# FNet layer 0 of a diffusion backbone: tokens transformed first, and all sixteen modulations of the second shift and scale as TensorE matmuls

## Chip, cores and metric

One core of a Trainium2 chip. The number that counts is the device time of one execution in microseconds (us). The kernel is written directly against the engines: TensorE (PE), VectorE (DVE), ScalarE (ACT), GpSimd (POOL), and SyncE (SP), which issues the large transfers. Each engine runs its own list of instructions in order and waits on semaphores.

## The reference

One inference step of a four-layer backbone on 128 context tokens and 512 latent tokens, 1024 channels, float32. Every layer is a token mixer (layer 0: Fourier, 1: pooling, 2: latent attention, 3: Fourier) followed by a gated ConvFFN. Both halves of a layer are modulated:

```
for i in range(DEPTH):
    sh1, sc1, g1, sh2, sc2, g2 = split(silu(cond) @ w_ada[i] + b_ada[i], 6)   # for c_ctx and for c
    h = rms_norm(x) * (1 + sc1) + sh1
    x = x + g1 * mixer_i(h)          # mixer 0: real part of FFT over (tokens, 256 channels), then @ w_fnet
    h = rms_norm(x) * (1 + sc2) + sh2
    x = x + g2 * conv_ffn(h, w_ffn_in[i], w_ffn_conv[i], b_ffn_conv[i], w_ffn_out[i])
```

Each of the six vectors has 1024 values, eight pieces of 128. So a layer has 48 *modulation units*: one unit is 128 outputs of `silu(cond) @ w_ada`, for both conditionings, and needs 512 KB of `w_ada`.

## The kernel before

`x` lies in SBUF channels by tokens (`x[128, 8, 644]`). All weights come through one stream of 512 KB units into a ring of four slots `raw0..raw3` (SP, L423 and L428). Unit n+4 is loaded once unit n was given back (`unit_done`), in the order of the stream. The products are float32 made of three TensorE passes: each operand is split into a rounded part `_hi` (ACT) and the rest `_lo` (POOL for weights, `cut`, L441; DVE for the others), and `product` (L563) issues hi*hi, hi*lo and lo*hi.

A modulation unit is computed in one of two ways. On DVE, `modulate` (L1802) multiplies the unit with `cond` and sums, once for each conditioning. On PE, `modulation` (L784, and the same loop inline at L1039) does eight matmuls of two columns each against `cond_columns`. DVE's output is added in place, PE's is copied from PSUM (`copy_modulations`).

Layer 0 runs in these stages, each engine's list written out by hand:

1. Sixteen units for shift and scale 1 (ten on DVE, six on PE) while DVE and ACT sum the squares of `x`. Then the statistics, and the normalised, modulated tokens `h_hi`, `h_lo` (`norm_half`).
2. `fnet`: PE does twelve units at once, "pe" units of the stream, before its first product. Then the channel transform of ten pieces (`STAGE1_ORDER`, outputs `freq`), and the token transform of nine pieces (`FOLDED`, outputs `folded`), with four more "pe" units between them and eight "dve" units on DVE.
3. The *fold projection*: eight steps m. DVE adds and subtracts two halves of a weight unit (`fold_unit`, L1910 and L1911), ACT rounds it, DVE makes the rest (`fold_lo`), PE does 27 passes (nine tiles of three, 324 or 320 columns), DVE updates `x` (`update_folded`, L1760). After each step PE does one "last" modulation unit (the eight of SC2).
4. The ConvFFN: 22 pairs of tiles in three parts of 8, 8 and 6 pairs, each part followed by a projection. With each pair DVE computes two modulation units of the next layer, and four more in the projection of part 1 (`EXTRA_PART`, `project_with_units`). All 48 units of layer 1 are made this way.

```
def fnet_units(layer):
...
        units += pe[:12]
...
    for m in range(KC):
        units += [("fold", m)] + ([("pe", MODS - LAST_PE + m)] if late else [])
```

Layers 1 to 3 and the ends of the program are not touched but for names.

## Time and profile before

| | us |
|---|---|
| median of 3 runs (2883.63 to 2891.56) | 2885.51 |
| the profiled execution | 2884.26 |
| its span, first to last instruction | 2882.5 |
| PE busy | 2637.6 (92%) |
| DVE busy | 1609.0 (56%) |
| ACT busy | 917.0 (32%) |
| POOL busy | 846.6 (29%) |

The profiled execution spends 1.8 us outside its span. The page gives each engine's busy time and the chain of work that ended last: 63% of it is on PE. PE's granted clock has two levels, shown as 1.00 (2.4 GHz) and 0.50 (1.2 GHz). The layers after the first FFN of this program do not differ between the two kernels, so the reading below stays with the first 250 us.

### The profile page before, as it was taken

The page shows a single profiled execution, that of the slowest core. Times are in us where ns is not written, and L with a number is a line of the kernel's source. Part 1 is how long each engine was busy: PE and PEld are TensorE (multiplying, and loading weights), DVE is VectorE, ACT ScalarE, POOL GpSimd, SP SyncE. Part 2 cuts the span into 40 slices and gives each one's busy share as a digit, 9 for nine tenths or more (in the row PEclk, how much of TensorE's full clock was granted, in tenths as well). Part 3 has the DMA queues.
Part 4 walks back from the last instruction along what each step waited for, and adds up shares of the span by engine and source line. Part 5 has one row for each costly group of instructions (what it writes and reads, how often), then busy time and mean ns, then how long its engine had stood idle before and what let it go on. Part 6 is the DMA issues. An engine that isn't in the chain of part 4 may idle for free.

```text
span 2882.5 us, 45477 instructions
## 1 busy us (share of the span) xinstructions
PE 2637.6 (92%) x17182; PEld 2589.7 (90%) x17182; DVE 1609.0 (56%) x2705; ACT 917.0 (32%) x1368; POOL 846.6 (29%) x414
## 2 busy tenths in 40 slices
PE   6889999996399999998888999999999888999997
PEld 6879999996399999988887889999999887999997
DVE  7478546576875475763543344754757776323235
ACT  3133223133332231343322333332323434323232
POOL 0012333334423333422111012233333302333332
PEclk9989999998699999999988899999999999999999
DMA  7433334342033343422100012333434311222222
GB/s 261 144 135 124 131 102 148 123 149 91 29 130 126 115 148 119 151 90 78 44 30 30 30 44 74 111 135 104 146 122 141 97 66 59 73 78 75 73 73 74
DMA packets 83858, 293.44 MB, mean 102 GB/s; under 512 B 9952, under 2 KB 13472, under 8 KB 83360
## 3 DMA queue, kind: packets, MB, share of 16 engines
q1 hardware_dynamic: 77184, 281.05, 28.9%
q10 hardware_dynamic: 6560, 10.79, 1.1%
q8 instruction: 81, 1.33, 0.2%
q14 instruction: 33, 0.27, 0.0%
HBM read 288.88 MB, written 2.93 MB: 101 GB/s over the span
## 4 chain that ended last, share of the span: by engine, by line
PE 63%; issue 16%; DVE 9%; POOL 5%; ACT 3%; DMA 2%; ACTq 0%; POOLq 0%; SPq 0%; DVEq 0%
PE acc L563 58%; POOL w_lo L441 4%; PE sacc L563 3%; PE sacc L784 2%; DMA raw<-in_stream 2%; DVE x L1760 1%; DVE rows L1789 1%; DVE pt_lo L1677 1%; POOL res_ffn L441 1%; DVE rows L1635 1%; POOL w_next L441 1%; DVE rows L1628 1%; DVE rows L1709 1%; DVE x L1700 1%; PE acc L980 1%
## 5 line engine op out<-in xcount | busy, mean ns | idle before, releaser
L441 POOL TENSOR_TENSOR w_lo<-raw,w_hi 128x1024 fp32r<-128x1024 f32 (+3 forms) x317 | 710.1, 2246 | 1729.4 <-ACT w_hi L1070 1729.4
L563 PE MATMUL acc<-h_hi,w_hi 128*128 128x322 f32 x2880 | 907.8, 315 | 90.9 <-DVE x L1780 28.6
L563 PE MATMUL acc<-h_lo,w_hi 128*128 128x322 f32 x2880 | 902.7, 313 | 0.0
L563 PE MATMUL acc<-h_hi,w_lo 128*128 128x322 f32 x2880 | 901.8, 313 | 0.0
L563 PEld LDWEIGHTS acc<-h_hi,w_hi 128*128 128x128 f32 x2880 | 549.6, 191 | 101.2 <-issue 77.4
L563 PEld LDWEIGHTS acc<-h_lo,w_hi 128*128 128x128 f32 x2880 | 552.5, 192 | 0.2
L563 PEld LDWEIGHTS acc<-h_hi,w_lo 128*128 128x128 f32 x2880 | 549.1, 191 | 0.0
L1070 ACT ACTIVATE w_hi<-raw 128x1024 fp32r<-128x1024 f32 (+2 forms) x283 | 293.0, 1036 | 784.7 <-PE acc L563 744.5
L1802 DVE SCALAR_TENSOR_TENSOR products<-raw,cond 128x1024 f32<-128x1024 f32 x324 | 440.5, 1396 | 12.2 <-ACT cond L1557 8.2
L1854 DVE SCALAR_TENSOR_TENSOR conv<-acc,conv_w,conv 128x644 f32<-128x644 f32 x168 | 149.4, 889 | 371.6 <-ACT conv L1293 267.8
L563 PE MATMUL acc<-g_hi,w_hi 128*128 128x322 f32 x1120 | 350.3, 313 | 5.8 <-POOL w_lo L441 5.8
L563 PE MATMUL acc<-g_hi,w_lo 128*128 128x322 f32 x1120 | 346.8, 310 | 0.0
L563 PE MATMUL acc<-g_lo,w_hi 128*128 128x322 f32 x1120 | 346.5, 309 | 0.0
L1780 DVE SCALAR_TENSOR_TENSOR x<-acc,mod,x 128x128 f32 (+5 forms) x198 | 74.9, 433 | 299.5 <-PE acc L563 299.5
L563 PEld LDWEIGHTS acc<-g_hi,w_hi 128*128 128x128 f32 x1120 | 210.5, 188 | 7.1 <-POOL w_lo L441 6.8
L563 PEld LDWEIGHTS acc<-g_lo,w_hi 128*128 128x128 f32 x1120 | 212.6, 190 | 0.3
L563 PEld LDWEIGHTS acc<-g_hi,w_lo 128*128 128x128 f32 x1120 | 210.9, 188 | 0.0
L1858 DVE SCALAR_TENSOR_TENSOR conv<-acc,conv_w,conv 128x644 f32<-128x644 f32 x168 | 149.4, 889 | 24.6 <-DVE conv L1854 22.2
L1298 ACT ACTIVATE g_hi<-gated 128x644 f32 (+1 forms) x88 | 65.4, 743 | 279.3 <-DVE gated L1864 279.3
L563 PE MATMUL acc<-g_hi,res_ffn 128*128 128x322 f32 x576 | 131.2, 311 | 6.1 <-DVE x L1700 6.1
L1868 DVE TENSOR_TENSOR g_lo<-gated,g_hi 128x644 f32 (+1 forms) x88 | 75.6, 859 | 88.8 <-ACT g_hi L1298 88.8
L1289 ACT ACTIVATE gated<-conv 128x644 f32<-128x644 f32 x88 | 65.7, 747 | 181.1 <-DVE conv L1858 181.1
(210 smaller groups left out, 3709.1 us busy)
## 6 DMA issues: line engine op xcount, KB each, us to landing
raw<-in_stream SPq DMA_DIRECT2D x536, 512.0 KB, 3.3
x<-in_x ACTq DMA_DIRECT2D x8, 322.0 KB, 10.2
cond<-in_cond ACTq DMA_DIRECT2D x2, 1024.0 KB, 5.8
inv_count<-in_inv_count ACTq DMA_DIRECT2D x1, 1328.0 KB, 5.7
out_y<-y ACTq DMA_DIRECT2D x2, 644.0 KB, 4.2
out_y<-y ACTq DMA_DIRECT2D x8, 161.0 KB, 2.5
rows<-in_rope ACTq DMA_DIRECT2D x1, 644.0 KB, 3.9
conv_w<-in_conv_w ACTq DMA_DIRECT2D x4, 88.0 KB, 2.3
```

Source lines behind the costliest of these rows:

```text
L441: done = nc.gpsimd.tensor_tensor(lo[:, cols], raw[slot][:, cols], hi[:, cols].bitcast(f32), ALU.subtract)
L563: done = nc.tensor.matmul(o, lhs[lp], rhs[rp][half], start=first and z == 0, stop=last and z == 2)
L784: done = nc.tensor.matmul(sacc[1][:, 0, 2 * column:2 * column + 2], raw[u % SLOTS][:, k * P:(k + 1) * P], cond_columns[:, k, :], start=k = ...
L980: done = nc.tensor.transpose(acc[p][:, z // 4, (z % 4) * P:(z % 4 + 1) * P], probs[(5 * hh + t) % 2][:, z * P:(z + 1) * P], ident[:])
L1070: nc.scalar.activation(hi, raw[slot][:, 0:size], ACT.Copy).then_inc(weights_hi, 1)
L1289: nc.scalar.activation(gated[:], conv[0][:, 1:W + 1], ACT.Silu).then_inc(silu_done, 1)
L1298: nc.scalar.activation(g_hi[:, ds(gate, 1), :].rearrange("p o t -> p (o t)"), gated[:], ACT.Copy).then_inc(g_rounded, 1)
L1780: done = nc.vector.scalar_tensor_tensor(xs, acc[pair][:, bank, p0:p0 + x1 - x0], gate(cond_), xs, ALU.mult, ALU.add)
L1802: nc.vector.scalar_tensor_tensor(out[z][:], raw[slot][:], 1.0, cond[:, z, :], ALU.mult, ALU.mult, accum_out=mod[:, layer % 2, ds(index, 1) ...
L1854: nc.vector.scalar_tensor_tensor(to, halves(banks[half]), tap(0), to, ALU.mult, ALU.add).then_inc(left_done, 1)
L1858: nc.vector.scalar_tensor_tensor(to, halves(banks[half]), tap(2), to, ALU.mult, ALU.add).then_inc(result_taken, 1)
L1868: nc.vector.tensor_tensor(g_lo[:, gc, :].rearrange("p o t -> p (o t)"), gated[:], g_hi[:, gc, :].rearrange("p o t -> p (o t)").bitcast(f32 ...
```

## The change

Layer 0 gets its own stream (`FIRST_UNITS`) and its own function on each engine (`first_fnet`); `fnet` remains for layer 3.

- Tokens also arrive tokens by channels (five units "token"). ACT squares, sums and rounds them, DVE takes the reciprocal and the rest: `token_hi`, `token_lo`. The token transform is done first, on normalised tokens without modulation, in eight tiles c (24 passes of 258 or 256 columns and 6 of 66 or 64 each). Scale 1 is applied when the result is taken out of PSUM (`g_hi`, `g_lo`); shift 1 enters only the zero frequency (`zero_freq`).
- The channel transform comes second, in nine tiles (eight of 6 passes, one of 24).
- Units: PE does 30 as before, now SC1 (8), two of SH1, four of G1, and all sixteen of SC2 and SH2, two ahead of each fold step. DVE does ten ahead of the FFN (was eighteen). The eight of G2 move to DVE in the FFN of layer 0, and push eight of layer 1's into more places: four in the projection of part 0, eight in that of part 1.
- The transfers of `x` and of the small constants are issued by ACT after the first three token units, no longer first. The Nyquist weights come by a DMA of their own.

```
-    for m in range(KC):
-        units += [("fold", m)] + ([("pe", MODS - LAST_PE + m)] if late else [])
+def first_units():
+    units = [("token", 1), ("table", 0), ("table", 1), ("token", 2), ("token", 3), ("table", 2), ("token", 4),
+             ("token", 0)]
+    units += pe(*range(SC1, SC1 + 4))
+    for j in range(4):
+        units += pe(SC1 + 4 + j) + dve(SH1 + j)
+    units += dve(SH1 + 4, SH1 + 5) + pe(SH1 + 6, SH1 + 7)
+    for j in range(4):
+        units += dve(G1 + 4 + j) + pe(G1 + j)
+    units += [("fold", m) for m in range(3)]
+    for m in range(KC):
+        units += pe(SC2 + m, SH2 + m)
+        units += [("fold", m + 3)] if m + 3 < KC else []
...
+EXTRAS = {0: {0: 4, 1: 8}, 1: {1: 4}, 2: {1: 4}}
...
+            def first_fnet():
+                pe.wait_ge(cond_ready, 1)
+                wait_unit(first_place("table", 0))
+                wait_unit(first_place("table", 1))
+                for t in T_ORDER:
+                    ...
+                    wait_unit(first_place("token", t))
+                    for c in range(3):
+                        token_tile(c, t)
+                    if t == 3:
+                        modulation(SC1, 0, 0)
+                    if t == 4:
+                        modulation(SC1 + 1, 0, 1)
+                modulation(SC1 + 2, 1, 0)
+                modulation(SC1 + 3, 1, 1)
+                for c in range(3, KC):
+                    pe.wait_ge(result_taken, c - 2)
+                    for t in T_ORDER:
+                        token_tile(c, t)
+                    if c < KC - 1:
+                        if c % 2:
+                            pe.wait_ge(mods_taken, c // 2)
+                        modulation(SC1 + 1 + c, (c + 1) // 2 % 2, (c + 1) % 2)
+                pe.wait_ge(mods_taken, 3)
+                modulation(SH1 + 6, 0, 0)
+                modulation(SH1 + 7, 0, 1)
+                for i, j in enumerate(C_ORDER):
+                    ...
+                    if i < 4:
+                        if i == 0:
+                            pe.wait_ge(mods_taken, 4)
+                        modulation(G1 + i, 1, i)
+                def late(m):
+                    if m == 0:
+                        pe.wait_ge(mods_taken, 5)
+                    modulation(SC2 + m, 0, m)
+                    modulation(SH2 + m, 0, KC + m)
+                pe.wait_ge(nyquist_split, 1)
+                fold_project(0, 0, late)
...
+                for c in range(KC):
+                    if c % 2 == 0:
+                        take_modulations(SC1 + c, 2, c // 2 % 2, 0, True).then_inc(mods_taken, 1)
+                        dve.wait_ge(mods_taken, c // 2 + 1)
+                    take_tokens(c)
+                    if c >= 3:
+                        unit(SH1 + c - 3)
+                unit(SH1 + KC - 3)
...
+                squares(1)
+                first_table(0)
+                rounded(1)
+                first_table(1)
+                squares(2)
+                rounded(2)
+                squares(3)
+                rounded(3)
+                first_table(2)
+                for c in range(KC):
+                    act.dma_start(x[:, c, :], a["x"][c]).then_inc(loaded, 16)
...
+                squares(4)
+                rounded(4)
```

The diff shows, in this order, the stream, PE's `first_fnet`, and the cores of DVE's and of ACT's.

**The fold step on PE.** The end of one step and the start of the next; `acc<-folded,w` are the products, `sacc1<-cond_columns,raw` is a modulation unit. Before:

```order
L563 MATMUL acc1<-folded0_52,w_hi1_59 128x320
L563 MATMUL acc1<-folded1_53,w_hi1_59 128x320
L563 MATMUL acc1<-folded0_52,w_lo1_61 128x320
L784 MATMUL sacc1<-cond_columns_69,raw3_57 128x2 x8
L563 MATMUL acc0<-folded0_52,w_hi0_58 128x324
L563 MATMUL acc0<-folded1_53,w_hi0_58 128x324
```

Changed:

```order
L635 MATMUL acc0<-folded0_52,w_hi0_60 128x320
L635 MATMUL acc0<-folded1_53,w_hi0_60 128x320
L635 MATMUL acc0<-folded0_52,w_lo0_62 128x320
L857 MATMUL sacc1<-cond_columns_74,raw2_58 128x2 x8
L857 MATMUL sacc1<-cond_columns_74,raw3_59 128x2 x8
L635 MATMUL acc1<-folded0_52,w_hi1_61 128x324
L635 MATMUL acc1<-folded1_53,w_hi1_61 128x324
```

Two units stand between two steps where one stood.

**The channel transform on PE**, changed kernel, from the end of its second tile (`acc0`) to the start of its third (`acc1`):

```order
L635 MATMUL acc0<-g_hi_86,tables0_101 128x320
L635 MATMUL acc0<-g_lo_87,tables0_101 128x320
L635 MATMUL acc0<-g_hi_86,tables1_102 128x320
L857 MATMUL sacc1<-cond_columns_74,raw3_59 128x2 x8
L635 MATMUL acc1<-g_hi_86,tables0_101 128x320
L635 MATMUL acc1<-g_lo_87,tables0_101 128x320
```

Each of the first four tiles has six such passes, and a unit follows it. Before, a piece of this transform had twelve passes of 256 columns, and a unit came after every fourth piece.

**ACT's first instructions**, before:

```order
L1567 DMA cond<-in_cond 128x2048
L1568 DMA cond_columns<-in_cond_columns 128x16
L1569 DMA b_ada<-in_b_ada 128x96
L1571 DMA x<-in_x 128x644 x8
L1573 DMA ident<-in_ident 128x128
L1573 DMA ones<-in_ones 128x128
L1573 DMA perm<-in_perm 128x128
L1573 DMA gains<-in_gains 128x26
```

Changed, from the rounding of the third token unit on (`token_lo,token_sum<-raw` is the squaring, `token_hi<-raw` the rounding):

```order
L1470 ACTIVATE token_hi<-raw_56,token_rstd 128x1024
L1194 ACTIVATE tables_101<-raw_57 128x650
L1490 DMA x<-in_x 128x644 x8
L1492 DMA ident<-in_ident 128x128
L1492 DMA ones<-in_ones 128x128
L1492 DMA perm<-in_perm 128x128
L1492 DMA gains<-in_gains 128x26
L1462 ACTIVATE token_lo,token_sum<-raw_58 128x1024
L1465 ACTIVATE token_rstd<-token_sum,eps 128x1
L1470 ACTIVATE token_hi<-raw_58,token_rstd 128x1024
```

The twelve issues of `x` and the constants stood in the first rows; they now stand ahead of the fourth token unit.

## Rows read from the trace of the kernel before

**Rows 1.** Busy time by stage: us, busy us and instructions of each engine, granted clock, DMA share, GB/s

```profile
91.40:136.40 45.00, 42.71 (x320) 42.25 (x320) 27.65 (x57) 10.14 (x28) 0.00 (x0) 0.92 0.38 130
...
145.30:193.10 47.80, 46.83 (x328) 46.68 (x329) 37.02 (x81) 12.49 (x14) 2.83 (x4) 0.95 0.46 161
193.10:209.20 16.10, 4.48 (x23) 3.08 (x22) 10.04 (x26) 6.60 (x12) 8.34 (x12) 0.64 0.29 98
...
507.00:563.00 56.00, 56.00 (x379) 56.00 (x379) 30.42 (x46) 9.23 (x9) 21.09 (x8) 1.00 0.35 114
```

**Rows 2.** Modulation units on PE: cold ones grouped (ns min/median/max), two warm ones

```profile
L784 PE MATMUL sacc<-cond_columns,raw x192: 345/352/373, 49.4 to 91.2; 128*128 128x2 f32 x192
...
151.46 1.84 PE L784 MATMUL sacc<-cond_columns,raw 128*128 128x2 f32 x16
...
157.24 1.84 PE L784 MATMUL sacc<-cond_columns,raw 128*128 128x2 f32 x16
```

**Rows 3.** Granted clock in four short stretches, same columns as rows 1

```profile
105.50:109.00 3.50, 2.85 (x25) 2.64 (x24) 3.50 (x9) 0.98 (x4) 0.00 (x0) 0.99 0.73 272
109.00:112.40 3.40, 3.40 (x18) 3.40 (x18) 2.09 (x4) 0.41 (x1) 0.00 (x0) 0.51 0.42 146
...
145.30:149.90 4.60, 4.58 (x17) 4.60 (x18) 2.43 (x3) 0.00 (x0) 0.00 (x0) 0.50 0.19 73
...
156.70:160.10 3.40, 3.40 (x29) 3.40 (x28) 1.73 (x3) 0.40 (x1) 0.00 (x0) 1.00 0.25 101
```

**Rows 4.** Timeline of PE: start, us, line, tiles, [idle before]

```profile
107.19 2.00 PE L784 MATMUL sacc<-cond_columns,raw 128*128 128x2 f32 x16 [0.66 <-DMA raw<-in_stream]
...
145.32 0.88 PE L563 MATMUL acc<-folded,w_hi 128*128 128x324 f32 x2 [8.89 <-issue]
```

**Rows 5.** Timeline of PE: passes of 256 columns, cold and warm

```profile
91.98 0.41 PE L563 MATMUL acc<-tables,h_lo 128*128 128x256 f32 x1
...
92.62 0.41 PE L563 MATMUL acc<-tables,h_lo 128*128 128x256 f32 x1
...
98.08 0.28 PE L563 MATMUL acc<-tables,h_lo 128*128 128x256 f32 x1
...
98.43 0.28 PE L563 MATMUL acc<-tables,h_lo 128*128 128x256 f32 x1
```

**Rows 6.** Timeline of ACT: two pieces of the token transform taken

```profile
118.97 0.44 ACT L1079 ACTIVATE folded<-acc 128x324 fp32r<-128x324 f32 x1 [1.32 <-PE acc L563]
...
120.74 0.44 ACT L1079 ACTIVATE folded<-acc 128x324 fp32r<-128x324 f32 x1 [1.32 <-PE acc L563]
```

**Rows 7.** Timeline of ACT (ACTq: its issues): the start, and the tables

```profile
2.17 4.34 ACTq L1571 DMA_DIRECT2D x<-in_x  x8
...
10.27 1.28 ACT L1556 ACT_TABLE_LOAD   x1 [10.27 <-issue]
...
45.60 2.64 ACT L1070 ACTIVATE tables<-raw 128x1024 fp32r<-128x1024 f32 x3 [4.23 <-DVE mod L1819]
```

**Rows 8.** Timeline of POOL: the rests of the three tables

```profile
46.73 6.18 POOL L441 TENSOR_TENSOR tables<-raw,tables 128x1024 fp32r<-128x1024 f32 x3 [46.28 <-ACT tables L1070]
```

**Rows 9.** DMA issues: KB each, median us from issue to landing

```profile
raw<-in_stream SPq DMA_DIRECT2D x536, 512.0 KB, 3.3
...
b_ada<-in_b_ada ACTq DMA_DIRECT2D x4, 48.0 KB, 3.6
...
cond_columns<-in_cond_columns ACTq DMA_DIRECT2D x1, 8.0 KB, 7.0
```

**Rows 10.** Chain that ended last, in order of time: one wait in the fold projection

```profile
177.77 5.63 DMA raw<-in_stream
```

**Rows 11.** Timeline of DVE: from the update of one fold step to the next fold unit

```profile
172.94 1.57 DVE L1760 SCALAR_TENSOR_TENSOR x<-acc,mod,x 128x65 f32<-128x65 f32 x5
...
177.13 0.68 DVE L1911 TENSOR_TENSOR sums<-raw 128x512 f32<-128x512 f32 x1
```

**Rows 12.** Timeline of ACT between the fold projection and the FFN

```profile
200.40 1.06 ACT L1070 ACTIVATE w_next<-raw 128x1024 fp32r<-128x1024 f32 x1 [3.21 <-DMA raw<-in_stream]
```

More of the change, by code:

```diff
@@ L146, in extra, with first_place, fnet_units, fnet_place @@
+FIRST_DVE = [u for kind, u in FIRST_UNITS if kind == "dve"]
+FIRST_MODS = G2
+assert N_FIRST % SLOTS == 0 and len(FIRST_PE) + len(FIRST_DVE) == FIRST_MODS
+def first_place(kind, i):
+    return FIRST_UNITS.index((kind, i))
+def fnet_units():
+    return [("table", j) for j in range(TABLE_UNITS)] + [("nyquist", 0)] + [("fold", m) for m in range(KC)]
+def fnet_place(kind):
+    return [u for u, (k, i) in enumerate(fnet_units()) if k == kind]
 def extra(layer, part):
-    return ADA_EXTRA if ada_in_ffn(layer) and part == EXTRA_PART else 0
+    return EXTRAS.get(layer, {}).get(part, 0)
@@ L472, in project @@
             def project(size, more):
-                places = [*WEIGHT_PLACES, 12, 13] if more else list(range(10))
+                places = WEIGHT_PLACES[more] if more else list(range(10))
                 for j in range(2, 10):
@@ L1873, in ffn @@
                     if part == 0:
[L1874 to L1876 removed]
+                        pair(0, 0, acc, layer == 0)
+                        pair(1 // turn, 1 % turn, sacc[::-1], layer == 0)
+                    start = 2 // turn if part == 0 else 0
+                    if part == 0 and layer == 0:
+                        for i in range(2, (MODS - FIRST_MODS) // 2):
+                            pair(i, 0, acc, True)
+                        start = (MODS - FIRST_MODS) // 2
+                    with dve.Fori(start, count // turn) as i:
                         for z in range(turn):
```

741 lines of the change are left out of this document (441 added, 300 removed).

## The prediction, made before the changed kernel ran

> **What bounds the kernel now.** I read the stages first, since only layer 0 changes. The FNet mixer takes 209 us before the FFN's first product. In the busy times by stage [rows 1] PE is full or nearly so in both transforms (42.71 of 45.0 us) and in the fold projection (46.83 of 47.8). The reader should see that PE is the engine to count, although a large part of its time in layer 0 is modulation units, eight matmuls of two columns each. The grouped row of L784 [rows 2] shows their price: the twelve units from 49.4 to 91.2 last 42 us, 3.5 us each, with no DMA or DVE in the way. In the fold projection the same unit lasts 1.84 us in the record and moves the list by 1.7 (a step is 157.24 - 151.46 = 5.78 us, 4.08 of products and 1.7 of a unit).
>
> The two prices are PE's two clocks. The granted clock [rows 3] is 0.5 from 109.0 to 112.4 and from 145.3 to 149.9. The passes of 256 columns show it directly: three take 92.62 - 91.98 = 0.64 us before 95 us and 98.43 - 98.08 = 0.35 later [rows 5]. (The clock column reads 1.00 before 95 us as well; the durations there are those of 1.2 GHz, so I go by the durations.) The clock rose after 3.9 us of products, not during 42 us of busy two-column matmuls. So a unit does not keep PE's clock up. One unit between long runs of products does no harm: at 156.7 to 160.1 the clock stays 1.00 [rows 3]. One unit and a gap of 0.66 us, at 107.19 [rows 4], cost it: it fell at 109.0 for 3.4 us. That is the fact on which this prediction turns.
>
> After the fold projection, 16.1 us pass to the FFN [rows 1], set by the transfer, on which ACT waits 3.21 us [rows 12]; nothing in this piece changes. From there on PE is full.
>
> **The sum.** It goes from the start to the last fold product (193.1 us now).
>
> *Start.* ACT issues three small transfers (2.1), loads a table (1.28, [rows 7]) and waits for `b_ada`: issued at 1.7 and 3.6 on the way [rows 9], so 5.3; with the 7.0 of `cond_columns` it would be 8. Then two issues, a second table load and the issue of `cond` bring it to 8. Squaring and root 1.4 (estimate: 2.64 us for 2698 columns of tables [rows 7] is 1.0 per 1024, and a little for the sum), a table 1.0: 10.4. POOL makes the rests of two tables at 2.3 each (6.18 for 2698 columns, [rows 8]). **First product at 16**, against 91.4. This is the gain: twelve cold units and the statistics no longer stand ahead.
>
> *Three token tiles, first part.* 54 passes, 18 cold at 0.213 and 36 at 0.118: 8.1 us, then a unit; 28. The fourth token unit is late. ACT reaches it at about 20 and then issues twelve transfers; at the start these took it from 2.17 to 10.27 [rows 7], 8.1 us. So 28; squaring 1.4, rounding 1.0 and DVE's rest 1.2 give **32**. PE waits 4 us for it and is cold again.
>
> *Rest of three tiles.* 18 wide passes cold 3.9, 18 narrow ones cold at 0.2, three units between 1.7 and 3.5, I take 8 for them: **47.5**. (Narrow, warm: a piece of the token transform is 12 wide and 3 narrow passes in 120.74 - 118.97 = 1.77 us [rows 6], less 12 x 0.118, leaves 0.11 each.)
>
> *Five tiles.* 24 x 0.118 + 6 x 0.11 = 3.5 each, and four units at 1.7: 24.3. A unit follows six narrow passes, so this is lighter than the fold step; I take three falls of the clock at 3.4 us and half speed, 1.7 each: **77**. Two more units, the second behind DVE's units in the ring: 8, **85**.
>
> *Channel transform.* Six passes of 320 columns are 0.9 us warm. Between single units there is too little, so cold: 6 x 0.27 + 3.5 = 5.1, four times, 20.4; four tiles without a unit, 5; the Nyquist tile, 24 passes, 4.5; small waits. **117**. The two transforms with their units thus end 19 us earlier than the 136.4 of now, and the folding of weights, 8.9 us of idle PE [rows 4], is done beside them: 28 us gained.
>
> *Fold projection.* Each step has 4.08 of products and now two units, 3.4: 7.5 us, 60 for eight, against 47.8. With 3.4 us of units in one piece I expect the clock to fall once a step. Price: the first step now, cold to 149.9, runs from 145.32 to 151.46, 6.14 instead of 4.08 [rows 2, 4]: 2.1 a step, 17. With 1 to 2 us of waits for the ring: **79**, so the last product at **196**, 3 us later than now.
>
> The bounds of this term: no fall gives 60; all units cold and each step's products as slow as the first's, 6.1 + 7.0 = 13.1, gives 105. I take one fall a step, since a single unit of 1.7 with a short gap already did it [rows 3, 4].
>
> The Trainium skill (TensorE: Matmul & The Clock Gate, "Why this matters for your kernels") asks, against drops of throughput, only that no long idle gaps stand between bursts of matmuls. PE is not idle here, and by that rule the clock would hold. The trace disagrees at 109.0. The rule's case is the first rival.
>
> *In the FFN.* DVE gets eight more units in layer 0, four in the projection of part 0 and four more in that of part 1. In part 1 DVE is busy 30.42 of 56 us with four units [rows 1]; four more at 2.4 make 40. PE covers it: nothing. Without that cover it would be at most 12 x 2.4 = 29 us. Copies and biases of the modulations, below 1 us each beside PE: nothing. SP's list has four units more before the FFN's end, in places where the ring waits anyway.
>
> Sum: +3 us on the profiled execution's 2884.26: **2887 us**. That execution lies 1.2 us under the median of the three runs.
>
> **Rivals.**
>
> *The clock holds (faster).* For it: it holds in the fold projection now, and the units still are matmuls. Against: rows 3 at 109.0. Then the channel transform is 4 x (0.9 + 1.7) instead of 20.4, minus 10; the falls of the five tiles, 5, are not paid, nor the 17 of the fold steps: 32 us less, 2855. If it holds in half the fold steps and the five tiles, minus 13: 2874.
>
> *The ring becomes the bound in the fold projection (slower).* Three units a step now pass through four slots, two before. The two units of step m+2 are loaded only when DVE gave back fold unit m+3, which is behind the update of x: 177.8 - 172.94 = 4.9 us after the products of step m [rows 11]. They land 3.3 us later if alone [rows 9], 5.6 as in the chain's wait at 177.77 [rows 10]. Two steps then take 4.9 + L + 7.5 us, a step 7.9 with L = 3.3 and 9.0 with 5.6. It decides from L = 2.6 on, when the clock is up; with a fall each step, 9.6, only when L exceeds 6.8 or the fall lies outside the wait. In the bad case both add: 9.0 + 2.1 = 11.1, 89 us, 10 more than my sum, and a second fall in the early tiles 2: 2899.
>
> *DVE's new units hold PE up in the FFN.* Up to 29 us, 2916. Against it the 16 us free in part 1. Small.
>
> *It does not start early.* If `b_ada` lands late and every token unit with it, the start moves by 3 to 5 us, but PE waits for the fourth token anyway. 2890, within the first case.
>
> **How the numbers follow.** About 0.3%, 8.7 us, is what a measurement of this kernel can tell from no change. The forecast, gain at the start given back by the fold projection, has 0.58: 2877 to 2894. The clock holding in whole or in half has 0.21, the ring 0.17, the FFN 0.04. Faster is 0.21, the same 0.58, slower 0.21. The range, 2868 to 2899, takes in the forecast, the half case and the usual price of the ring; the full case of the first rival and the far end of the others are left out.
>
> **What would show it.** Right: the first product near 16 us; a wait of PE of some 4 us before the fourth token; the transforms done near 117; granted clock 0.5 in one or more short stretches in each fold step, and a mean step of 9 to 10 us; the last fold product at 190 to 200; FFN unchanged. Wrong: a clock of 1.00 through the fold projection with steps of 7.5 to 8 us (first rival); idle PE ahead of the units with the ring named as releaser, longer than 1 us in each step (second); PE gaps at the projections of parts 0 and 1 (third).

## The result, and the profile after

| | changed | before |
|---|---|---|
| median of 20 runs | 2876.24 us (2868.0 to 2890.24) | 2886.8 us (2873.74 to 2892.93) |
| ratio, with 95% interval | 0.9975 [0.9963, 0.9987] | |
| profiled execution, span | 2875.66, 2873.9 us | 2884.26, 2882.5 us |

The changed kernel is 0.25% faster, by some 7 us going by the ratio. The forecast was 2887, no change. The time lies in the range, but on the side to which I gave 0.21.

The forecast was made of stages of layer 0, so these are read first. Busy time by stage of the changed kernel, with the columns of [rows 1]: three token tiles, five token tiles, channel transform, fold projection, the piece up to the FFN, and part 1 of the FFN.

```profile
15.80:49.60 33.80, 29.27 (x172) 28.79 (x173) 9.89 (x32) 16.09 (x28) 3.95 (x2) 0.75 0.77 265
49.60:84.00 34.40, 32.59 (x223) 32.51 (x222) 18.80 (x48) 7.54 (x21) 0.00 (x0) 0.75 0.37 123
84.00:118.30 34.30, 31.91 (x145) 31.54 (x145) 18.29 (x39) 5.63 (x11) 0.00 (x0) 0.56 0.61 214
118.30:198.50 80.20, 77.21 (x474) 76.24 (x472) 41.18 (x90) 13.03 (x15) 2.79 (x4) 0.79 0.44 148
198.50:212.10 13.60, 2.52 (x5) 1.24 (x5) 8.52 (x23) 6.52 (x12) 7.70 (x12) 0.67 0.15 56
510.10:566.30 56.20, 56.20 (x379) 56.20 (x378) 45.93 (x61) 9.24 (x9) 25.63 (x8) 1.00 0.44 151
```

The fold projection took 80.2 us where I had summed 79. PE's clock, 0.95 there before [rows 1], is 0.79. A mean of 0.79 between 1.00 and 0.50 is 42% of the 80.2 us at half speed, 34 us, and these cost half their length: 17 us, the term that I had put down for it. It came about in another way than I had it: the clock fell in five of the eight steps and not in all, and stayed low for 6.8 us each time. One such stretch, and one of the steps at full clock:

```profile
121.10:127.90 6.80, 6.80 (x28) 6.80 (x29) 2.99 (x4) 0.00 (x0) 0.00 (x0) 0.50 0.53 177
138.20:147.30 9.10, 9.10 (x71) 9.00 (x69) 5.59 (x12) 1.80 (x2) 0.00 (x0) 1.00 0.33 115
```

Lines of the timeline of PE in the changed kernel: the first product, the first unit, the first product of the fourth token, then in the fold projection two pairs of units (x32) and a single one (x16), and the first product of the FFN.

```profile
15.82 0.77 PE L635 MATMUL acc<-tables,token_hi 128*128 128x258 f32 x2 [15.82 <-POOL tables L501]
27.68 2.48 PE L857 MATMUL sacc<-cond_columns,raw 128*128 128x2 f32 x16 [2.68 <-DMA raw<-in_stream]
31.02 0.80 PE L635 MATMUL acc<-tables,token_hi 128*128 128x258 f32 x2 [0.86 <-DVE token_lo L2161]
...
118.34 4.33 PE L857 MATMUL sacc<-cond_columns,raw 128*128 128x2 f32 x32
129.02 4.74 PE L857 MATMUL sacc<-cond_columns,raw 128*128 128x2 f32 x32
...
148.18 1.95 PE L857 MATMUL sacc<-cond_columns,raw 128*128 128x2 f32 x16 [0.71 <-DMA raw<-in_stream]
...
212.06 0.61 PE L635 MATMUL acc<-h_hi,w_hi 128*128 128x322 f32 x1 [6.29 <-issue]
```

The FFN starts at 212.06, 2.87 us later than before, where 3 was forecast. So in this profile layer 0 did what I said, and the program still ended 8.6 us earlier. The gain lies far behind layer 0, in code that the change leaves as it was: at the statistics of layer 2's q (1366.05 us before, 1368.12 now) the changed kernel is still 2.1 us behind.

**Where it comes from.** The costliest groups of POOL, each form of instruction by itself (busy us, mean ns). First a second profile of the kernel before, then one of the changed kernel:

```profile
L441 POOL TENSOR_TENSOR w_lo<-raw,w_hi 128x1024 fp32r<-128x1024 f32 x249 | 640.3, 2572 | 1274.8 <-ACT w_hi L1070 1274.8
L441 POOL TENSOR_TENSOR res_ffn<-raw,res_ffn 128x768 fp32r<-128x768 f32 x24 | 47.6, 2013 | 4.2 <-ACT res_ffn L1070 4.2
L441 POOL TENSOR_TENSOR w_next<-raw,w_next 128x256 fp32r<-128x256 f32 x32 | 23.2, 759 | 13.7 <-ACT w_next L1070 13.7
L441 POOL TENSOR_TENSOR res_mla<-raw,res_mla 128x1024 fp32r<-128x1024 f32 x5 | 11.9, 2403 | 30.2 <-ACT res_mla L1070 30.2
```

```profile
L501 POOL TENSOR_TENSOR w_lo<-raw,w_hi 128x1024 fp32r<-128x1024 f32 x249 | 650.5, 2613 | 1265.9 <-ACT w_hi L1194 1265.9
L501 POOL TENSOR_TENSOR res_ffn<-raw,res_ffn 128x768 fp32r<-128x768 f32 x24 | 39.7, 1679 | 5.5 <-ACT res_ffn L1194 5.5
L501 POOL TENSOR_TENSOR w_next<-raw,w_next 128x256 fp32r<-128x256 f32 x32 | 20.3, 670 | 11.1 <-ACT w_next L1194 11.1
L501 POOL TENSOR_TENSOR res_mla<-raw,res_mla 128x1024 fp32r<-128x1024 f32 x5 | 9.9, 2015 | 38.6 <-ACT res_mla L1194 38.6
```

The same instructions on the same shapes: 2013 ns and 1679, 759 and 670, 2403 and 2015. Of these only `w_lo` did not become quicker. What differs is where the tiles lie. The change places three small tiles that I had read over, ahead of all tiles but `x`, `h`, `raw`, the four weight tiles and the small constants:

```
+        token_sum, token_rstd = place("token_sum", [P, 5]), place("token_rstd", [P, 5])
+        zero_freq = place("zero_freq", [P, 2, KC])
         g_at = at[0]
```

That is 26 words, 104 bytes. The sizes add up to a start of `g_hi`, and with it of `tables`, `res_mla`, `w_next` and four of the six `res_ffn`, at 60 modulo 64 bytes before and at 36 now. The other two `res_ffn` and `w_nyq` start at 28 before and at 4 now. `raw`, `w_hi` and `w_lo` start at 0 in both.

### The profile page after: what moved, and what is told of

It reads as the page before. It is cut to its first block, busy times and chain, and to the rows that moved or that the text cites. A ratio compares the mean times of both kernels' runs of the same rounds, so it can differ in the third digit from the quotient of the medians.

```text
span 2873.9 us, 45480 instructions
## 1 busy us (share of the span) xinstructions
PE 2643.5 (92%) x17235; PEld 2597.9 (90%) x17235; DVE 1593.3 (55%) x2692; ACT 918.8 (32%) x1369; POOL 840.7 (29%) x414
## 4 chain that ended last, share of the span: by engine, by line
PE 69%; issue 13%; DVE 9%; POOL 4%; ACT 3%; DMA 1%; ACTq 0%; POOLq 0%; DVEq 0%; SPq 0%
PE acc L635 63%; POOL w_lo L501 3%; PE sacc L635 3%; PE sacc L857 2%; DMA raw<-in_stream 1%; DVE x L1935 1%; DVE pt_lo L1853 1%; DVE rows L1804 1%; DVE rows L1811 1%; DVE rows L1964 1%; POOL w_next L501 0%; ACT w_hi L1194 0%; DVE scratch L2308 0%; DVE h_lo L1827 0%; POOL res_ffn L501 0%
## 5 line engine op out<-in xcount | busy, mean ns | idle before, releaser
L501 POOL TENSOR_TENSOR w_lo<-raw,w_hi 128x1024 fp32r<-128x1024 f32 (+3 forms) x317 | 719.4, 2274 | 1826.0 <-ACT w_hi L1194 1826.0
L1977 DVE SCALAR_TENSOR_TENSOR products<-raw,cond 128x1024 f32<-128x1024 f32 x304 | 428.4, 1446 | 2.6 <-issue 2.5
L1955 DVE SCALAR_TENSOR_TENSOR x<-acc,mod,x 128x128 f32<-128x128 f32 (+5 forms) x198 | 75.0, 434 | 269.0 <-PE acc L635 269.0
```

Of the source, the lines that this page charges most:

```text
L501: done = nc.gpsimd.tensor_tensor(lo[:, cols], raw[slot][:, cols], hi[:, cols].bitcast(f32), ALU.subtract)
L1955: done = nc.vector.scalar_tensor_tensor(xs, acc[pair][:, bank, p0:p0 + x1 - x0], gate(cond_), xs, ALU.mult, ALU.add)
L1977: nc.vector.scalar_tensor_tensor(out[z][:], raw[slot][:], 1.0, cond[:, z, :], ALU.mult, ALU.mult, accum_out=mod[:, layer % 2, ds(index, 1) ...
```

## The experiments

Sixteen more runs were made, three of them of the two kernels as they are. "Rest" is the time from the first FFN product to the end of the profiled execution's span. The expectations count to PE's last product instead, some 10 us less.

| kernel | median, us | ratio to before [95%] | FFN starts | rest |
|---|---|---|---|---|
| before, as above | 2886.8 | 1 | 209.2 | 2673.3 |
| changed, as above | 2876.24 | 0.9975 [0.9963, 0.9987] | 212.1 | 2661.8 |
| before_again | 2884.03 | 0.9992 [0.9981, 1.0003] | 211.5 | 2676.5 |
| before_pad4 | 2882.83 | 0.9992 [0.9982, 1.0002] | 209.3 | 2672.9 |
| before_pad128 | 2888.26 | 1.0004 [0.9993, 1.0015] | 214.4 | 2678.3 |
| after_old_places | 2885.16 | 0.9990 [0.9975, 1.0004] | 214.1 | 2682.2 |
| before_late | 2891.94 | 1.0015 [0.9998, 1.0032] | 213.8 | 2669.8 |
| before_pad (104 bytes) | 2879.54 | 0.9968 [0.9953, 0.9983] | 209.9 | 2673.9 |
| after_again | 2879.7 | 0.9973 [0.9959, 0.9987] | 212.1 | 2667.4 |
| after_third | 2875.44 | 0.9969 [0.9953, 0.9986] | 208.5 | 2663.4 |
| after_w32 | 2880.2 | 0.9981 [0.9965, 0.9998] | 209.5 | 2666.6 |
| after_late | 2883.01 | 0.9982 [0.9965, 0.9998] | 214.3 | 2677.3 |
| split_fold | 2888.21 | 1.0004 [0.9985, 1.0023] | 215.0 | 2668.0 |
| no_sh2 | 2871.71 | 0.9949 [0.9934, 0.9964] | 199.8 | 2661.6 |
| after_w36 | 2874.56 | 0.9966 [0.9952, 0.9980] | 210.1 | 2659.8 |
| before_w36 | 2873.32 | 0.9958 [0.9943, 0.9973] | 212.7 | 2659.0 |

The ratios are to the kernel before on the same chip, whose medians were 2885.4 to 2889.2. scan1 and scan2 were executed once each, for their profiles. A profile is one execution and its time lies where it may in the spread of 15 to 20 us: for the whole time the medians and ratios count.

### Is it scatter?

**before_again** and **after_again**: both kernels unchanged.

> The kernel before, unchanged, for the scatter of its parts. In the first pair of profiles layer 0 of the changed kernel ended 2.9 us later (first FFN product 212.06 against 209.19), and code that the change doesn't touch was 11 us shorter after it, 6 of them in layer 2's attention (1422 to 1556 against 1422 to 1561). Theory A (scatter): the granted clock falls in other places in each execution, so a second profile of the same kernel differs from the first by 3 us or more in attention and by 5 or more in all that follows 695 us. Theory B (real): two profiles of this kernel agree within 1.5 us in each of these, and the changed kernel is shorter there each time. Time ratio to before: 1.000 within 0.002.

> The changed kernel, unchanged, a second profile. Ratio to before 0.9975 again, within 0.0015. Theory A: its attention and layer 3 are not 6 and 5 us shorter than in the profiles of before, but anywhere between those of the two kernels. Theory B: 7 to 11 us shorter than before from 695 us on, again. Theory C (layer 0 quicker in most executions than in the one profiled): the first FFN product at 200 to 208 this time instead of 212.

The ratio came again, 0.9973, and before against itself gave 0.9992. The rest was 2676.5 and 2667.4. Theory C is out: the FFN started at 212.1 once more. Attention (1422 to 1561 us in the first profile) is the clearest piece. Between the same two products, in the first and the second profile of before, then of the changed kernel (columns of [rows 1]):

```profile
1422.10:1561.40 139.30, 121.78 (x737) 113.04 (x737) 50.66 (x127) 40.35 (x100) 15.56 (x8) 0.85 0.10 31
```

```profile
1424.70:1564.50 139.80, 122.25 (x736) 113.70 (x736) 50.71 (x127) 40.44 (x100) 15.55 (x8) 0.84 0.10 31
```

```profile
1424.00:1556.60 132.60, 114.92 (x737) 106.67 (x736) 50.49 (x127) 39.93 (x99) 15.56 (x8) 0.89 0.10 33
```

```profile
1424.30:1557.30 133.00, 115.00 (x737) 106.73 (x737) 50.55 (x127) 40.01 (x100) 15.57 (x8) 0.89 0.10 33
```

The work of DVE, ACT and POOL is the same; PE's busy time and clock differ. Theory A asked for 3 us between two profiles of one kernel here; it was 0.5 and 0.4. That looked like theory B. But a third profile of the changed kernel (after_third, below) took 136.4 us in this stretch, 3.8 more than the first.

### The place of the tiles

**before_pad**, no instruction differs from before:

```
+        place("pad", [P, 26])
         g_at = at[0]
```

> The kernel before with 104 unused bytes (26 words) placed in SBUF ahead of g_hi, so that all that lies behind (g, tables, res_ffn, w_next, the attention's tiles) moves to where the changed kernel has it; no instruction differs. In two profiles of each kernel POOL's rest of 768 columns of res_ffn took 2.01 us before and 1.68 after, that of 256 columns of w_next 0.76 and 0.67, of 1024 columns of res_mla 2.40 and 2.01, while w_lo took 2.57 and 2.61. The changed kernel adds three small tiles of 104 bytes at that place. Theory E (placement): POOL's times become the changed kernel's (1.68, 0.67, 2.01), the code from the first FFN product on takes 2651 to 2658 us instead of 2662 to 2666, attention (1422 to 1561) 133 instead of 139, and the median falls by 6 to 10 us, to 2875 to 2881. Rival (the tiles' places do nothing on the path; the gain comes with the new order of layer 0 and its units): POOL may be quicker, the median stays within 3 us of before.

**after_old_places**, the changed kernel with its three tiles behind all others:

```
-        token_sum, token_rstd = place("token_sum", [P, 5]), place("token_rstd", [P, 5])
-        zero_freq = place("zero_freq", [P, 2, KC])
...
+        end_at = at[0]
+        token_sum, token_rstd = (place(f"token_{n}", [P, 5], f32, end_at + 20 * j) for j, n in enumerate(("sum", "rstd")))
+        zero_freq = place("zero_freq", [P, 2, KC], f32, end_at + 40)
```

> The changed kernel with its three small tiles (token_sum, token_rstd, zero_freq, 104 bytes) placed at the end of the allocation, so that all other tiles lie where they lay before. Theory E: POOL's times become those of before (2.01, 0.76, 2.40), the time from the first FFN product on is 2662 to 2666 us, and the median rises to 2885 to 2892, by what my forecast for layer 0 says above before. Rival: the median stays at 2876 to 2881.

The groups of POOL in before_pad:

```profile
L442 POOL TENSOR_TENSOR res_ffn<-raw,res_ffn 128x768 fp32r<-128x768 f32 x24 | 39.6, 1678 | 5.8 <-ACT res_ffn L1071 5.8
L442 POOL TENSOR_TENSOR w_next<-raw,w_next 128x256 fp32r<-128x256 f32 x32 | 20.2, 669 | 13.8 <-ACT w_next L1071 13.8
```

104 unused bytes give the kernel before the changed kernel's POOL and 0.9968, all of the change's gain. The changed kernel with the old places has POOL's old times (2017 ns for `res_ffn`) and 0.9990: its interval holds 1. It also reaches into that of the changed kernel, up to 0.9987, so the ratio of this run alone decides nothing; the times set right for the clock, below, do. One part of the expectation failed: before_pad's attention took 136.1 us and not 133, and its rest was 2673.9, no shorter than the 2673.3 of before; the profiled execution, at 2885.63 us, lay 6 us above the median of its runs. The gain of before_pad is seen in the median of its twelve runs, not in its profile.

**before_pad4** and **before_pad128**: the same line with `[P, 1]` and `[P, 32]`.

> The kernel before with 4 unused bytes ahead of g_hi instead of 104. What lies behind starts at 60 modulo 64 bytes in the kernel before, at 36 in the changed kernel, and here at 0, as raw, w_hi and w_lo do. POOL's rest takes 2.57 us for 1024 columns of w_lo (0 against 0), 2.40 for res_mla (60 against raw's 0) and 2.01 with 36. Theory G (the place of POOL's operands relative to each other, modulo 64, sets its speed, worst where they are equal): res_mla takes 2.5 to 2.6 us here, res_ffn 2.05 to 2.2, w_next 0.76 to 0.79, and the median is that of before or up to 3 us above. Rival (a tile that starts off a 64-byte line is what costs): both become quicker than with 36, below 2.0 and 1.67, and the median falls by more than the 9.7 us of the 104 bytes.

> The kernel before with 128 unused bytes at the same place: everything behind moves, but keeps its 60 modulo 64. Theory G: POOL's times stay at those of before (2.40 for res_mla, 2.01 for res_ffn, 0.76 for w_next) and the median within 2 us of before. Rival (any move of these tiles by some hundred bytes does it, or the gain of before_pad is scatter): times or median as in before_pad, 2.01 / 1.68 / 0.67 or 6 to 10 us less.

Neither changed POOL's times (`res_ffn` 2024 ns in the first, `res_mla` 2405) nor the ratio, 0.9992 and 1.0004. So 104 bytes matter for what they do to the remainder, not for moving the tiles, and with these two runs the place of the tiles is shown as the cause of the gain. That POOL's speed carries it is likely, not shown by itself: DVE's busy time also fell in before_pad, to 1601.1 us from 1608.0 to 1609.6 in the five profiles of the kernel before with POOL's old times. But 0 was no worse than 60, and the distance as I had it in theory G is not all.

**after_w32**: 8 unused words ahead of `w_hi` and 8 ahead of `g_hi`.

> The changed kernel with 32 unused bytes ahead of w_hi, and 32 more ahead of g_hi: raw starts at 0 modulo 64, w_hi and w_lo at 32, the rest at 36 as in the changed kernel. Theory G: the rest of 1024 columns of w_lo takes 2.0 to 2.1 us instead of 2.61, all 249 of them 510 to 530 us instead of 651. PE's waits that end with w_lo, 27 us in the changed kernel's profile, shrink by a fifth to a third: 5 to 9 us less, 2867 to 2874 us, the fastest so far. Rival: w_lo stays at 2.5 to 2.6 (then the place of the output, or something else, decides), and the median within 2 us of the changed kernel.

**after_third**, run beside it: the changed kernel unchanged.

> The changed kernel once more, as the measure for after_w32 on the same chip. Ratio to before 0.9965 to 0.9985; from the first FFN product on 2651 to 2658 us in the profile, first product at 205 to 214.

`w_lo` stayed at 2606 ns, so 32 modulo 64 is not a quick place, and theory G fell. The median did not fall: 2880.2 beside 2875.44 for after_third, with intervals that overlap. after_third did what I expected: 2653.4 us from the first FFN product to PE's last one.

**scan1** and **scan2** put single tiles at many places within one program:

```
-        res_ffn = [[place(f"res_ffn{i}{p}", [P, 6 * P], f32r, res_at[i] + 24 * P * p) for p in range(2)] for i in range(3)]
+        res_ffn = [[place(f"res_ffn{i}{p}", [P, 6 * P], f32r, res_at[i] + 24 * P * p + ((0, 4), (28, 64), (64, 92))[i][p]) for p in range(2)] for i in range(3)]
...
+        mla_shift = (0, 4, 12, 28, 44)
-        res_mla = [[place(f"res_mla{i}{p}", [P, UNIT], f32r, e_at + 4 * UNIT * (2 * i + p)) for p in range(2)]
+        res_mla = [[place(f"res_mla{i}{p}", [P, UNIT], f32r, e_at + 4 * UNIT * (2 * i + p) + mla_shift[i]) for p in range(2)]
```

In scan2 the shifts of `res_ffn` are ((0, 28), (28, 32), (36, 64)) and `mla_shift` is (32, 36, 48, 52, 60).

> The changed kernel with single tiles shifted. Start modulo 64 bytes, rounded part and rest alike: the five res_mla at 36, 40, 48, 0 and 16. Of res_ffn, rounded part / rest: tile 0 at 36 / 40, tile 1 at 0 / 36, tile 2 at 36 / 0; tiles 3 to 5 as before. raw is at 0 throughout. Theory G (distance to raw): a time that grows smoothly towards 0 and 60, so 36 and 40 quick (2.0), 48 and 16 between, 0 slow (2.4). Theory H (only starts at 4 modulo 32, or modulo 16, are quick): 36 at 2.0, all others 2.4. For res_ffn: if the rounded part's place decides (it is read), tiles 0 and 2 stay quick (1.55 undisturbed) and 1 is slow (1.84); if the rest's (it is written), tile 1 is quick and the others slow; if both must be alike, all three are slow.

> As scan1 with other offsets: res_mla at 4, 8, 20, 24 and 32; res_ffn tile 0 at 36 / 0, tile 1 at 0 / 4, tile 2 at 8 / 36. Theory H: 4 and (if it is modulo 16) 20 quick at 2.0 us, the others 2.4. Theory G: 20, 24 and 32 quick, 4 and 8 slow.

Timeline of POOL in scan1. Five `res_mla`, start modulo 64 bytes 36, 40, 48, 0, 16:

```profile
1751.38 2.01 POOL L502 TENSOR_TENSOR res_mla<-raw,res_mla 128x1024 fp32r<-128x1024 f32 x1 [31.12 <-ACT res_mla L1195]
1753.35 2.00 POOL L502 TENSOR_TENSOR res_mla<-raw,res_mla 128x1024 fp32r<-128x1024 f32 x1
1755.31 2.39 POOL L502 TENSOR_TENSOR res_mla<-raw,res_mla 128x1024 fp32r<-128x1024 f32 x1
1757.66 2.39 POOL L502 TENSOR_TENSOR res_mla<-raw,res_mla 128x1024 fp32r<-128x1024 f32 x1
1761.45 2.40 POOL L502 TENSOR_TENSOR res_mla<-raw,res_mla 128x1024 fp32r<-128x1024 f32 x1 [1.39 <-ACT res_mla L1195]
```

And in scan2, at 4 and 8, at 20 and 24 (two in a line, 2.00 us each), and at 32:

```profile
1743.83 3.95 POOL L502 TENSOR_TENSOR res_mla<-raw,res_mla 128x1024 fp32r<-128x1024 f32 x2 [35.48 <-ACT res_mla L1195]
...
1747.74 3.95 POOL L502 TENSOR_TENSOR res_mla<-raw,res_mla 128x1024 fp32r<-128x1024 f32 x2
...
1754.88 2.40 POOL L502 TENSOR_TENSOR res_mla<-raw,res_mla 128x1024 fp32r<-128x1024 f32 x1 [3.19 <-ACT res_mla L1195]
```

Quick are 36, 40, 4, 8, 20, 24; slow are 48, 0, 16, 32, and 60 from the kernel before. Modulo 16 that is 4 and 8 quick, 0 and 12 slow. Theory H had the period but not the 8. The split tiles, scan1, tile 1 (rounded part at 0, rest at 36) and tile 2 (rounded part at 36, rest at 0) of `res_ffn`:

```profile
1228.58 2.44 POOL L502 TENSOR_TENSOR res_ffn<-raw,res_ffn 128x768 fp32r<-128x768 f32 x1
...
1233.11 1.54 POOL L502 TENSOR_TENSOR res_ffn<-raw,res_ffn 128x768 fp32r<-128x768 f32 x1 [2.10 <-ACT res_ffn L1195]
```

Tile 1 took 2.14 us in the changed kernel, tile 2 1.55. So the tile that is read decides, and where the result goes does not. scan2 agrees: rounded part at 0 slow (2.43), at 8 or 36 quick (1.54), wherever the rest was.

The Trainium skill (SBUF — State Buffer, Specifications (TRN2)) gives SBUF lines of 16 bytes and says that each crossing to a new line is paid for. The period of 16 found here agrees with such lines. Why 4 and 8 past the other input are quick and 12 is not, neither the page nor a run here tells.

**after_w36** and **before_w36**: 9 unused words ahead of `w_hi` and 7 (33 in before) ahead of `g_hi`.

> The changed kernel with w_hi and w_lo at 36 modulo 64 (36 unused bytes ahead of them, 28 ahead of g_hi, so that the rest keeps its 36). If the place of the tile alone decides, w_lo's rest of 1024 columns takes 2.0 us undisturbed instead of 2.40 (mean 2.2 instead of 2.61), the 256 columns 0.64 instead of 0.73, and PE's waits that end with w_lo (27 us) shrink by a fifth: 2869 to 2874 us. Rival: w_lo stays at 2.4 and the median at 2875 to 2880; or it becomes quicker and the median does not move, since the falls of the clock take it back.

> The kernel before with w_hi, w_lo and all behind them at 36 modulo 64. If the place decides and nothing else: quick rests throughout as in after_w36, and a median 5 us below that of the 104 bytes alone: 2870 to 2876. Rival: w_lo unchanged, 2877 to 2881.

```profile
L503 POOL TENSOR_TENSOR w_lo<-raw,w_hi 128x1024 fp32r<-128x1024 f32 x249 | 548.6, 2203 | 1364.6 <-ACT w_hi L1196 1364.4
L503 POOL TENSOR_TENSOR w_nyq<-raw,w_nyq 128x1024 fp32r<-128x1024 f32 x1 | 2.0, 2003 | 16.8 <-ACT w_nyq L1196 16.8
L580 POOL TENSOR_TENSOR w_nyq<-nyquist_raw,w_nyq 128x1024 fp32r<-128x1024 f32 x1 | 2.5, 2526 | 10.0 <-ACT w_nyq L1500 10.0
```

POOL works 102 us less on `w_lo`. The last two lines show that the distance of the two inputs counts and not the place of one: `w_nyq` starts at 4 modulo 64 in both. `raw` starts at 0, a distance of 4 modulo 16, and takes 2003 ns. `nyquist_raw` lies behind the new pad and starts at 36, a distance of 0 modulo 16, and takes 2526. In the changed kernel, where `nyquist_raw` starts at 0, the same instruction took 2147.

The time followed little. before_w36 has 2873.32 us, ratio 0.9958, and after_w36 2874.56, 0.9966; the changed kernel, run beside after_w32, had 2875.44, 0.9969. The intervals overlap, so no order among these three is shown. Both medians lie below every median with the old places, and before_w36 does it without the change to layer 0.

### How a quicker POOL reaches PE

Some of it is direct. Ahead of layer 3: DVE, POOL and PE in the second profile of before, then POOL and PE in before_pad:

```profile
2288.89 2.81 DVE L1651 SCALAR_TENSOR_TENSOR h_lo<-rows,mod,h_hi 128x128 fp32r<-128x128 f32 x2
```

```profile
2288.95 4.95 POOL L441 TENSOR_TENSOR tables<-raw,tables 128x1024 fp32r<-128x1024 f32 x2 [27.57 <-ACT tables L1070]
```

```profile
2295.41 0.56 PE L563 MATMUL acc<-tables,h_hi 128*128 128x256 f32 x2 [4.33 <-issue]
```

```profile
2286.20 4.18 POOL L442 TENSOR_TENSOR tables<-raw,tables 128x1024 fp32r<-128x1024 f32 x2 [29.13 <-ACT tables L1071]
```

```profile
2291.88 0.61 PE L564 MATMUL acc<-tables,h_hi 128*128 128x256 f32 x2 [3.65 <-issue]
```

A pair of DVE's instructions that takes 0.67 us elsewhere takes 2.81 while POOL makes the tables' rests, and with POOL's 4.18 instead of 4.95 PE waits 0.68 us less. The Trainium skill (SBUF — State Buffer, Who interferes with whom) says that a VectorE instruction with two inputs in SBUF and a GpSimd one that reads SBUF keep each other waiting. The trace agrees.

Some goes by the clock. Behind POOL's rests of `w_next` PE waited 2.20 us at 1804.63 in before and 1.80 at 1809.17 in before_pad. Right behind that wait the clock fell in the one and held in the other. First before, then before_pad, the columns of [rows 1]:

```profile
1805.50:1808.70 3.20, 3.20 (x14) 3.20 (x14) 3.17 (x3) 0.53 (x1) 1.21 (x2) 0.50 0.00 0
```

```profile
1810.10:1813.30 3.20, 3.20 (x24) 3.20 (x23) 3.00 (x3) 0.51 (x1) 0.88 (x2) 1.00 0.00 0
```

PE did 14 matmuls in one and 24 in the other. The two executions differ in more than this wait, but the other profiles say the same. In all six with the old places (before, before_again, before_pad4, before_pad128, before_late, after_old_places) PE waited 2.18 to 2.21 us here and the clock fell right behind it. In the twelve others it waited 1.75 to 1.80, and the clock fell in one only, scan1. The fall lasts 3.4 us, so it costs at most 1.7.

*How much is clock.* The record has the mean granted clock of every execution. An estimate from it: time x (1 - clock) is what the low clock can have cost at most, and time x clock is the rest, which no fall of the clock can explain. In means, against the kernel before in the same session, with 95% intervals:

| | time, us | clock's part | the rest of it |
|---|---|---|---|
| before_pad | -10.1 | -5.8 ± 4.2 | -4.3 ± 1.6 |
| before_pad4 | -2.4 | -3.6 ± 2.2 | +1.2 ± 1.5 |
| before_pad128 | +2.8 | +1.9 ± 3.3 | +0.9 ± 1.5 |
| before_w36 | -12.1 | -5.0 ± 4.2 | -7.1 ± 1.4 |
| after_again | -6.9 | +35.9 ± 3.3 | -42.8 ± 1.2 |
| after_third | -8.2 | +33.8 ± 4.7 | -42.0 ± 1.2 |
| after_old_places | -2.8 | +36.2 ± 4.8 | -38.9 ± 1.6 |
| after_w36 | -9.9 | +36.3 ± 4.5 | -46.2 ± 1.6 |

The changed kernel has more low clock in layer 0, and the column shows the kernel before at 1.00 during its twelve cold units, so the rows of the changed kernel are read against each other only. In both kernels the new places take 3 to 4 us off the part without the clock, and `w_lo` at 36 takes off some 3 to 4 more. These differences are clear of the scatter. What the clock adds to it is 6 us in before_pad, with a wide interval, and is not seen in the changed kernel.

**before_late** and **after_late** test how far shifts alone move the clock's falls; before the statistics of q, 8 and 2 times

```
+                    nc.tensor.matmul(sacc[0][:, 0, 0:2], ones[:], sum_q[:, 0:2], start=True, stop=True)
```

> The kernel before with eight matmuls of two columns more (2 to 3.4 us) ahead of the statistics of q in layer 2 (near 1369 us), so that attention starts so much later. Theory F (where PE's clock falls depends on small shifts of the program): in both profiles of before the clock falls at 1423 and 1447 and in none of the four of the changed kernel, though the code is the same. With the shift these falls go or move: attention, 139 us from 1422 to 1561, becomes 132 to 136, and the added 2 to 3.4 us cost nothing in sum or bring a gain. Rival: attention stays at 139 within 1 us, and the whole time rises by the added 2 to 3.4 us.

> The changed kernel with two matmuls of two columns more (0.4 to 0.9 us) at the same place. Theory F: the program stood just on the good side of a fall, and so small a shift brings the falls at 1423 and 1447 back: attention 137 to 140 us instead of 132.5, the median up by 4 to 7 us. Rival: up by 0.4 to 0.9 us, attention as in the changed kernel.

Attention in before_late and in after_late:

```profile
1429.90:1562.90 133.00, 115.12 (x736) 106.70 (x735) 50.52 (x127) 40.02 (x99) 15.56 (x8) 0.89 0.10 33
```

```profile
1430.80:1571.40 140.60, 123.47 (x735) 114.83 (x735) 50.60 (x127) 40.26 (x99) 15.59 (x8) 0.83 0.09 31
```

The stretch took 140.6 us with two matmuls more, after 133 in the changed kernel, and 133.0 with eight more, after 139.5 in the kernel before. That looks like theory F, but it does not show it. Both executions came to the added matmuls some 6 us later than the first profile of their kernel: at 1372.03 against 1366.05, and at 1373.97 against 1368.12, where the additions themselves moved the list by 1.95 and 0.87 us. What else differed before them may have moved the falls. What is shown is that unchanged code takes 132.6 to 140.6 us here, by where the clock falls, so this stretch alone could not have told placement from luck. Nor does it stand for the whole: after_third, with nothing added, took 136.4 us in it, and before_w36, the fastest by its rest, 139.1. The medians moved little: after_late, 0.9982 against 0.9969 to 0.9975, is 2 to 4 us slower than the changed kernel where I expected 4 to 7, within what the intervals allow. before_late is 2.7 us above its before, which is the rival's 2 to 3.4, and no gain. An edit made to hit a good moment in one profile did not carry over to all executions.

### The units in layer 0

**split_fold**, the unit of SH2 within the step:

```
                         for z, j in enumerate(tiles):
+                            if layer == 0 and (part, z) == (0, 4):
+                                modulation(SH2 + m, 0, KC + m)
...
                     modulation(SC2 + m, 0, m)
-                    modulation(SH2 + m, 0, KC + m)
```

> Changed kernel, but in each fold step the unit of SH2 stands after the fourth of the nine tiles of products and only that of SC2 between two steps. My reading (PE's clock falls once a step because 3.6 us of units stand in one piece): pieces of 1.8 us between 2 us of products keep 1.00, a step is 4.1 + 3.6 = 7.7, or up to 8.8 where the ring binds, against 10.0; layer 0 ends 10 to 18 us earlier, the time falls by 10 to 18 us against the changed kernel (2858 to 2866). Rival (the clock falls with every unit, however short the piece, or the ring binds at once): a step stays at 9.5 to 10.5, the time within 4 us.

Two stretches of its fold projection:

```profile
122.00:158.40 36.40, 36.40 (x156) 36.40 (x154) 11.89 (x27) 4.24 (x5) 0.00 (x0) 0.50 0.36 130
```

```profile
182.00:197.00 15.00, 15.00 (x119) 15.00 (x118) 8.89 (x22) 3.48 (x4) 2.02 (x3) 1.00 0.56 182
```

And units of its timeline in each:

```profile
121.87 3.41 PE L857 MATMUL sacc<-cond_columns,raw 128*128 128x2 f32 x16
...
135.95 3.41 PE L857 MATMUL sacc<-cond_columns,raw 128*128 128x2 f32 x16
...
186.03 1.84 PE L857 MATMUL sacc<-cond_columns,raw 128*128 128x2 f32 x16
...
193.59 1.84 PE L857 MATMUL sacc<-cond_columns,raw 128*128 128x2 f32 x16
```

Neither theory held throughout. With the clock up, the same unit of two neighbouring steps stands at 186.03 and 193.59, a step of 7.56 us, as in my reading. With the clock down, 121.87 to 135.95, a step is 14.08. The clock fell in the first step, at 120.8, stayed low for 37.5 us and rose at 158.3 amid the same pattern; it fell once more at 168.6, behind a single unit before which PE had waited 0.46 us for the ring, for 10.2 us. What made it rise at 158.3 no run shows. The FFN started at 215.0, and the median, 2888.21, is 8 to 10 us above the changed kernel's by the ratios. In these two profiles, one of each, the pairs of the changed kernel lost the clock more often, five times, but for 6.8 us each; the single units lost it twice, and for longer: mean clock 0.79 against 0.71 over the projection. So the unbroken products of a step were worth more than short pieces of units.

**no_sh2**:

```
-                for k in range(KC):
+                for k in range(KC - 1 if SH2 <= unit < SH2 + KC else 0, KC):
```

> Changed kernel, but each unit of SH2 is one matmul instead of eight: seven eighths of these outputs' sums are left out (of the matmuls, k = 0 to 6). Prices the second unit of a fold step. My reading: without it the clock holds, a step is 4.1 + 1.8 + 0.2 = 6.1 us and the ring binds at some 7 to 8: layer 0 ends 16 to 28 us earlier. Rival (no fall of the clock is tied to the pair): a step loses only the unit's 1.8 or less, 14 us. In both the whole time should fall by what layer 0 loses; if it falls by less, the layers behind it give it back.

The FFN started at 199.8, 12.3 us earlier, less than I expected and near the rival's 14. Two pairs of its timeline:

```profile
137.00 3.72 PE L857 MATMUL sacc<-cond_columns,raw 128*128 128x2 f32 x18 [2.58 <-DMA raw<-in_stream]
...
154.84 4.00 PE L857 MATMUL sacc<-cond_columns,raw 128*128 128x2 f32 x18 [2.43 <-DMA raw<-in_stream]
```

With the second unit's work gone the ring is the bound. Behind each of these two gaps the pair ran at the low clock: 3.72 and 4.00 us, where it takes 2.06 at full clock. By the ratios the whole kernel became 6 to 8 us faster than the changed one (0.9949, from six runs, against 0.9969 to 0.9975) for the 12.3.

## Why the prediction was right and wrong

*Right, in the profile it was made for.* First product 16, measured 15.82. The fourth token at 32, measured 31.02; PE waited there 3.5 us in two pieces, 2.68 for a late unit and 0.86, for the 4 that I gave it. Five tiles to 77, measured 78.4 (the unit behind them starts there). Transforms done at 117, measured 118.3. Fold projection 79, measured 80.2, with the clock at 0.79. FFN at 212, measured 212.06. In part 1 DVE is busy 45.93 us, where I estimated 40, and PE is full, so the four more units there cost nothing.

*Right sums of wrong terms.* Part of this agreement is luck. The five tiles began early, at 45.9 and not 47.5, and took 32.5 us and not 29.4: the clock was low in five stretches and not three. In the fold projection I had eight falls at 2.1 us each, 17 in all; there were five of 6.8 us at half speed, at 3.4 each, 17 in all. The sign "granted clock 0.5 in one or more short stretches in each fold step" was therefore not seen: three steps held 1.00.

*The rivals.* The first, that the clock holds, came true in three steps of eight and gained nothing, since each fall lasted longer. The ring (second rival) cost PE four waits of 0.65 to 0.84 us, 2.9 in all, where my sum has 1 to 2; it became the bound only in no_sh2. The third, DVE in the FFN, cost nothing: from the first FFN product to the start of the next layer's statistics (694.25 before, 695.25 now) the changed kernel needs 483.2 us, before 485.1.

*Wrong.* The step that failed is "Sum: +3 us on the profiled execution's 2884.26": it takes all that lies behind layer 0 as unchanged. What stands ahead of the prediction says that the layers after the first FFN do not differ. Their instructions and the order of these are indeed the same; the tiles they work on had moved by 104 bytes. In its place the runs showed 0.9968 for this move by itself, -9 us, and 0.9990 for the rest of the change, -3 us with an interval from -7 to +1. Their product, 0.9958, lies below the 0.9969 to 0.9975 of the changed kernel, but within what these intervals allow.

*The size of layer 0's own part.* With the old places it is 0.9990 against 1; with 104 bytes in both it is 0.9969 to 0.9975 against 0.9968; with quick weights as well, 0.9966 against 0.9958. The forecast of +3 us, 0.1%, lies among these; no ratio here can tell it from zero. The start of the FFN alone scatters from 209.2 to 214.4 in the seven profiles with the old layer 0, and from 208.5 to 214.3 in the nine with the new one unaltered. The means are 211.5 and 211.6 us. So 2.87 us in one pair was agreement within the scatter, and the means speak for nothing rather than 3.

*Open.* Why a distance of 4 or 8 bytes is quick and 12 is not. Which waits make up the 3 to 4 us that the clock does not explain: one was read, 0.68 us ahead of layer 3. And how much the clock adds.

## What to carry to other kernels

A change that adds a small tile ahead of others moves all of them. Compare the mean duration of each form of instruction between the two profiles before explaining a gain by the edit; where an unchanged instruction changed its time, add the same unused bytes to the kernel before and run that. Let the second SBUF input of a float32 GpSimd subtraction like POOL's start 4 or 8 bytes past the first modulo 16: here that took 17% off it at no cost. Other types and operations were not tried.

Where narrow matmuls such as the modulation units must stand among products, keep the runs of products unbroken. Spread evenly, the units gave the shortest step with the clock up (7.56 us) and the longest with it down (14.08), and a slower kernel.

Read more than one profile of a kernel before a stretch is called faster, and split the times by the granted clock: here the part without it had intervals of ±1.5 us where the whole had ±3.5.

## What the hardware showed that I had not expected

- POOL's subtraction of 1024 float32 columns from SBUF took 2.00 us or 2.40 us undisturbed, by the distance of its two inputs modulo 16 bytes, whatever the place of the output.
- The same list of products and units ran 14.08 us a step at a granted clock of 0.50 and 7.56 at 1.00, in one execution, and stayed at 0.50 for 37.5 us with PE busy throughout.
- A wait of PE that shrank from 2.2 to 1.8 us took a fall of the clock with it: six profiles of six had it with the long wait, one of twelve with the short one.
